# The output projection of a decoder step: from fp32 products to three rounded products, with the residual stream returned later

## The chip, the cores and the metric

The kernel runs on one core of a Trainium2 chip, as one launch. The metric is the device time of the launch in microseconds (us), which is the median of three runs. TensorE multiplies matrices, VectorE, ScalarE and GpSimd do the rest of the arithmetic, and SyncE issues most of the transfers between HBM (the chip's main memory) and SBUF (the memory on the core).

## The reference

A two-layer decoder trunk is computed for 512 prompt tokens and for 8 samples of 4 tokens, 544 rows in all. Every layer projects the normed rows, runs a recurrent memory (mLSTM) and a sparse attention on them, and merges the two by one output projection `w_out` of 1024 by 1024, whose product is added to the residual stream `x`. A gated FFN follows.

```python
for l in range(DEPTH):                       # DEPTH = 2
    mq, mk, mv, mo, mi, mf, aq, ak, av, iq, ik, iw = project(x, g_mix[l], w_in[l])
    m_out, state = mlstm_mixer(mq, mk, mv, mo, mi, mf, ...)      # 512 columns
    a_out = dsa_prompt(...)  # or dsa_sample(...), with paged keys and values; 512 columns
    mix = jnp.concatenate([m_out, a_out], axis=-1)
    x = x + mix @ w_out[l]
    g, u = jnp.split(rmsnorm(x, g_ffn[l]) @ w_gate_up[l], 2, axis=-1)
    x = x + (jax.nn.silu(g) * u) @ w_down[l]
```

## The kernel before

All engines' programs are written out by hand, in order, one function each (`sync_layer`, `pool_layer` for GpSimd, `act_layer` for ScalarE, `tensor_layer`, `vector_layer` for VectorE), and a loop runs them twice, once for each layer. Semaphores are the only thing that holds one engine back for another. `eng.wait_ge(s, n)` waits until semaphore `s` has reached `n`, and `.then_inc(s, 1)` raises it when an instruction is done.

The rows are kept transposed: 8 blocks of 128 features (`KT = 8`) on the partitions, and `T = 544` rows along the free axis, as `x[:, k, t]`. A feature tile of an output is 128 output features by 544 rows. It is summed in two PSUM banks, in two halves of 272 rows.

**Plain fp32 products.** `feature_tile` (line 1064) takes the fp32 weights as they lie in the slab buffer `ring` and the fp32 rows, 8 blocks x 2 halves. In the profile each such product shows as two weight loads and two matmuls, so a tile has 32 matmul records. The 8 tiles of the output projection and the first tile of the down projection are made in this way.

**Three rounded products.** Every other large product splits each operand into a high part, rounded to the type fp32r, and a low part, the whole minus the high part. It sums high x high, high x low and low x high. A tile then has 8 x 3 x 2 = 48 products. `token_chunk` (line 1033) and `conv_tile` (L1049) of the input projection do so, `split_tile` (L1099) of the FFN and `down_tile` (L1080). The weights of the convolution tiles are split by GpSimd: `cast_feature` (L621) writes the high part, `low` (L626) writes the low part over the slab. Those of the FFN are split by VectorE (L1916, L1917).

**Memory.** `ring`, `proj`, `xn`, `cq`, `qk2` and `R4` are fp32 buffers, and `ring_low`, `h_high`, `x_high`, `x_low`, `w_split_even` and `w_split_odd` are the same places in the same order under the type fp32r. `K_PLACE` and `V_PLACE` say where the keys and values of each of the 8 samples are put, 8 pages each.

**Around the output projection.** For each layer the order is:

1. The mixed rows are put into `mixv`, which is `xn`. TensorE turns four heads of the memory (L1437) and four blocks of the attention (`turn_out`, L1426). ScalarE copies the heads out of PSUM (L960) and VectorE the attention (L1888). Both first wait until the results of the layer are stored (`s_stored`).
2. The sample attention runs: `turn_keys` (L1451), `sample_logits` (L1459), `turn_probs`, and `sample_values` (L1489, L1490), which raises `s_s_pv` once for each sample. SyncE loads keys (L552), GpSimd values (L704). After the last keys SyncE issues the return of `x` from its parking place in HBM (L585, 2.2 MB), then the two slabs of `w_out` (L495): slab 8 once all keys are turned, slab 9 once two samples have their values.
3. VectorE scales the last values (L1901), TensorE turns them (L1512), VectorE copies the eight heads of the sample rows into `mixv` (L1905) and raises `s_mix_ready`.
4. TensorE makes the 8 tiles (L1064). After tile m, from m = 2, it adds the sum of squares of tile m-2 (`sum_squares`, L1109). VectorE adds each tile to `x` (L1930) and scales it (L1932), ScalarE squares it (L991). After tile 6 VectorE splits the first FFN weights.

The code that sets the path into step 4 is this:

```python
pe.wait_ge(s_mix_ready, 1)
for m in range(8):
    feature_tile(8 + m // 4, OUT0 + m, P * (m % 4), mixv)
    if m >= 2:
        sum_squares(s_sq2, m - 2)
```

## Time and profile before

| | |
|---|---|
| median of 3 runs | 2156.34 us (2147.86 to 2165.62) |
| the profiled execution, its own time | 2154.16 us |
| its span, first to last instruction | 2152.2 us |
| TensorE busy | 1988.0 us (92%) |
| weight loads of TensorE | 1609.7 us (75%) |
| VectorE busy | 1175.7 us (55%) |
| ScalarE busy | 445.9 us (21%) |
| GpSimd busy | 457.9 us (21%) |
| mean granted clock of TensorE | 0.939 |

The span is 2.0 us shorter than the execution's own time. PE is TensorE's matmuls, PEld its weight loads, DVE is VectorE, ACT is ScalarE, POOL is GpSimd and SPq the queue of SyncE's transfers. The granted clock is a share of the full 2.4 GHz; at 0.5 it is 1.2 GHz. Matmuls are pipelined, so the duration of one record is longer than the distance from one start to the next, and a tile is best read from the start of its first matmul to the start of what comes after it.

### The profile page before, as it was taken

How to read it: one execution, taken by the hardware profiler on the slowest of the kernel's cores; microseconds unless marked ns; L12 is line 12 of the kernel's file. 1: busy time of each engine (PE TensorE's matmuls, PEld its weight loads, DVE VectorE, ACT ScalarE, POOL GpSimd, SP SyncE). 2: the span in 40 equal slices, each digit the busy share in tenths (PEclk: the TensorE clock that was granted, in tenths of full speed). 3: DMA queues.
4: the chain of work that ended last, by engine and by line, in shares of the span. 5: the costliest groups of instructions: out<-in, count | busy, mean ns of one | idle time of the engine just before them, and what ended most of it. 6: DMA issues, size and time to landing. Idle time of an engine off the chain costs nothing. (4 is left out here: it accounts for less than half of the span.)

```text
span 2152.2 us, 31183 instructions
## 1 busy us (share of the span) xinstructions
PE 1988.0 (92%) x11900; PEld 1609.7 (75%) x11900; DVE 1175.7 (55%) x2074; ACT 445.9 (21%) x940; POOL 457.9 (21%) x436
## 2 busy tenths in 40 slices
PE   6999998887999999999969999987889999999997
PEld 5765576744478999989957656766444899999897
DVE  3295975578114454555425779656770155454653
ACT  2123233323202000040022233233331020000400
POOL 2453340034100121200026435201240012121000
PEclk9998988878999999999979999887889999999999
DMA  3320320107511322233232213102172122322332
GB/s 120 120 81 9 93 68 1 55 27 217 183 40 41 116 80 79 79 81 82 55 106 81 81 33 97 40 1 81 53 238 110 40 79 79 108 89 67 81 82 69
DMA packets 183537, 174.32 MB, mean 81 GB/s; under 512 B 30946, under 2 KB 159234, under 8 KB 182866
## 3 DMA queue, kind: packets, MB, share of 16 engines
q1 hardware_dynamic: 178002, 157.55, 23.4%
q0 software_dynamic: 5376, 14.69, 2.2%
q8 instruction: 96, 1.57, 0.3%
q14 instruction: 63, 0.52, 0.1%
HBM read 158.03 MB, written 14.17 MB: 80 GB/s over the span
## 5 line engine op out<-in xcount | busy, mean ns | idle before, releaser
L1099 PE MATMUL psum<-x_high,w_split_even 128*128 128x272 f32 x1408 | 238.5, 289 | 2.3 <-DVE x_low L1938 2.3
L724 POOL TENSOR_TENSOR rawr<-rawr,pen 128x544 f32<-128x544 f32 x44 | 98.4, 2237 | 658.7 <-ACT rawr L1002 658.7
L1099 PE MATMUL psum<-x_high,w_split_odd 128*128 128x272 f32 x1408 | 237.6, 288 | 0.0
L1080 PE MATMUL psum<-h_high,w_split_even 128*128 128x272 f32 x1232 | 204.6, 287 | 1.7 <-issue 1.7
L1099 PEld LDWEIGHTS psum<-x_high,w_split_even 128*128 128x128 f32 x1408 | 199.8, 188 | 3.3 <-issue 3.1
L1099 PEld LDWEIGHTS psum<-x_high,w_split_odd 128*128 128x128 f32 x1408 | 199.6, 188 | 0.0
L1080 PEld LDWEIGHTS psum<-h_high,w_split_even 128*128 128x128 f32 x1232 | 173.4, 188 | 2.5 <-issue 2.5
L1033 PE MATMUL psum<-h_high,x_high 128*128 128x512 f32 (+1 forms) x400 | 168.5, 421 | 0.0
L1033 PE MATMUL psum<-h_high,x_low 128*128 128x512 f32 (+1 forms) x400 | 162.1, 405 | 0.0
L1033 PE MATMUL psum<-ring_low,x_high 128*128 128x512 f32 (+1 forms) x400 | 161.3, 403 | 0.0
L1942 DVE TENSOR_TENSOR rawr<-psum,pen 128x544 f32<-128x544 f32 x44 | 31.9, 725 | 228.1 <-PE psum L1099 215.0
L626 POOL TENSOR_TENSOR ring_low<-ring,h_high 128x512 fp32r<-128x512 f32 (+1 forms) x96 | 153.8, 1603 | 7.7
L1916 DVE CAST w_split_even<-ring 128x256 fp32r<-128x256 f32 (+1 forms) x198 | 98.6, 498 | 99.3 <-PE psum L1080 78.4
L1099 PE MATMUL psum<-x_low,w_split_even 128*128 128x272 f32 x704 | 145.1, 288 | 0.0
L1099 PE MATMUL psum<-x_low,w_split_odd 128*128 128x272 f32 x704 | 145.1, 288 | 0.0
L1002 ACT ACTIVATE rawr<-rawr 128x544 f32<-128x544 f32 x44 | 29.2, 663 | 470.8 <-DVE rawr L1942 470.8
L1064 PE MATMUL psum<-xn,ring 128*128 128x272 f32 x512 | 121.2, 397 | 3.4 <-DVE xn L1905 3.4
L1917 DVE TENSOR_TENSOR w_split_even<-ring,w_split_even 128x256 fp32r<-128x256 f32 (+1 forms) x198 | 119.6, 604 | 6.8
L1064 PEld LDWEIGHTS psum<-xn,ring 128*128 128x128 f32 x512 | 98.2, 192 | 24.4 <-DVE xn L1905 3.9
L1099 PEld LDWEIGHTS psum<-x_low,w_split_odd 128*128 128x128 f32 x704 | 110.6, 189 | 0.0
L1099 PEld LDWEIGHTS psum<-x_low,w_split_even 128*128 128x128 f32 x704 | 110.6, 189 | 0.0
L1033 PEld LDWEIGHTS psum<-h_high,x_high 128*128 128x128 f32 (+1 forms) x400 | 71.6, 179 | 51.7 <-issue 28.9
(375 smaller groups left out, 3575.8 us busy)
## 6 DMA issues: line engine op xcount, KB each, us to landing
ring<-in_w_gate_up_dram SPq DMA_DIRECT2D x44, 1024.0 KB, 7.4
ring<-in_w_in_dram SPq DMA_DIRECT2D x14, 2048.0 KB, 7.9
ring<-in_w_down_dram SPq DMA_DIRECT2D x16, 1408.0 KB, 6.9
ring<-in_w_out_dram SPq DMA_DIRECT2D x4, 2048.0 KB, 8.5
cq<-in_cache_k_dram SPq DMA_DIRECT2D x48, 128.0 KB, 2.0
ring<-in_cache_k_dram SPq DMA_DIRECT2D x48, 128.0 KB, 2.8
x_spill<-x SPq DMA_DIRECT2D x2, 2176.0 KB, 13.3
x<-x_spill SPq DMA_DIRECT2D x2, 2176.0 KB, 11.6
```

The source lines that it names most:

```text
L626: pool.tensor_tensor(out, whole, high.bitcast(F32), ALU.subtract).then_inc(s_w_low, 1)
L724: pool.tensor_tensor(sig(f), sig(f), rstd_ffn.rearrange("p (h t) -> p h t", h=2), ALU.mult).then_inc(s_silu_scaled, 1)
L1002: act.activation(sig(f), sig(f), ACT.Silu).then_inc(s_gate_silu, 1)
L1033: mm = pe.matmul(ps(t)[0:r, :], v[:, k, c:c + r], w, start=(k == 0 and q == 0), stop=(k == KT - 1 and q == 2))
L1064: mm = pe.matmul(out[:, 512 * hf:512 * hf + HALF], w[:, k, c:c + P], src[:, k, HALF * hf:HALF * hf + HALF], start=(k == 0), stop=(k == nk ...
L1080: mm = pe.matmul(out[:, 512 * hf:512 * hf + HALF], down_part(c, w)[:, cols], v[:, HALF * hf:HALF * hf + HALF], start=(k == 0 and q == 0), ...
L1099: mm = pe.matmul(out[:, 512 * hf:512 * hf + HALF], w_part(f, w)[:, k, u, :], v[:, k, HALF * hf:HALF * hf + HALF], start=(k == 0 and q == 0 ...
L1916: step(dve.tensor_copy(high, whole))
L1917: return dve.tensor_tensor(low, whole, high.bitcast(F32), ALU.subtract)
L1942: dve.tensor_tensor(sig(f), halves(FFN0 + 2 * f), rstd2, ALU.mult).then_inc(s_gate_scaled, 1)
```

## The change

- The output projection is made of three rounded products for each block and half (`out_tile`), 384 for a layer in place of 128 fp32 ones.
- Its weights are split by GpSimd (`low_out`), through three buffers in `h_high` (`out_high`). The split of tile m waits for tile m-3.
- The mixed rows lie as a high part (`mix_high`, in `qk2`) and a low part (`mix_low`, in `xn`). ScalarE writes the high parts out of PSUM, for the attention too, and VectorE subtracts them to write the low parts. TensorE's reuse of the PSUM banks now waits for the low parts. For the sample rows VectorE does both, eight small casts and then eight small subtractions.
- `qk2` is thus taken, and so the keys and values that lay there move: the keys of sample 5 to `x`, its values to `R4`, and the values of sample 2 to `x`. The return of `x` from HBM therefore waits for the third sample value and stands behind both slabs of `w_out` in SyncE's queue.
- The FFN's weight buffers change places (`w_part`), and three semaphores become one (`s_prepared`).

```diff
+        mix_high = w_split_even[:, :].rearrange("p (k t) -> p k t", k=KT)
+        mix_low = xh
...
+                sp.wait_ge(s_out_free, OUT0)
                 load_keys(5)
...
-                sp.wait_ge(s_x_parked, 16)
-                sp.dma_start(x[:, :], x_spill).then_inc(s_x_parked, 16)
                 sp.wait_ge(s_kt_turned, 4 * DB)
                 load_slab(8)
                 sp.wait_ge(s_s_pv, 2)
                 load_slab(9)
+                sp.wait_ge(s_x_parked, 16)
+                sp.wait_ge(s_s_pv, 3)
+                sp.dma_start(x[:, :], x_spill).then_inc(s_x_parked, 16)
...
+                def low_out(m):
+                    i = 8 + m // 4
+                    if m % 4 == 0:
+                        slab_arrived(pool, i)
+                    if m == 0:
+                        pool.wait_ge(s_s_log, DB)
+                    elif m == 2:
+                        pool.wait_ge(s_s_pv, 5)
+                    elif m >= 3:
+                        pool.wait_ge(s_out_done, OUT0 + m - 2)
+                    pool.tensor_copy(out_high(m), feature_cols(slab_view(i), m)).then_inc(s_w_high, 1)
+                    low(FEAT0 + 8 + m, feature_cols(slab_view(i), m), out_high(m), feature_cols(slab_low(i), m))
...
-                act.wait_ge(s_c_new, MH)
-                act.wait_ge(s_stored, 16 * STORES)
+                attention_high(0)
+                attention_high(1)
                 for h in range(MH):
                     act.wait_ge(s_mix_turned, h + 1)
-                    act.activation(mixv[:, h, :], ps(2 * (h % 2), 2)[:, 0:T], ACT.Copy).then_inc(s_mix_copied, 1)
+                    act.activation(mix_high[:, h, :], ps(2 * (h % 2), 2)[:, 0:T], ACT.Copy).then_inc(s_mix_copied, 1)
+                attention_high(2)
+                attention_high(3)
...
+                def out_tile(m):
+                    high, low = out_high(m), feature_cols(slab_low(8 + m // 4), m)
+                    pe.wait_ge(s_w_low, FEAT0 + 8 + m + 1)
+                    out = slot(OUT0 + m)
+                    for k in range(KT):
+                        for q, (w, v) in enumerate(((high, mix_high), (high, mix_low), (low, mix_high))):
+                            for hf in range(2):
+                                mm = pe.matmul(out[:, 512 * hf:512 * hf + HALF], w[:, k, :], v[:, k, HALF * hf:HALF * hf + HALF],
+                                               start=(k == 0 and q == 0), stop=(k == KT - 1 and q == 2))
+                    mm.then_inc(s_out_done, 1)
...
                 for h in range(QH):
-                    ins = dve.tensor_copy(mixv[...], ps(1)[...])
+                    whole, high, low = sample_part(h)
+                    ins = dve.tensor_copy(high, whole)
+                step(ins)
+                for h in range(QH):
+                    whole, high, low = sample_part(h)
+                    ins = dve.tensor_tensor(low, whole, high.bitcast(F32), ALU.subtract)
                 ins.then_inc(s_mix_ready, 1)
```

On TensorE the output projection begins behind the last turn of the sample values. Before the change its rows are these (`xn` holds the mixed rows, `ring` the weights):

```order
L1512 MATMUL psum<-con,proj 128x128 [waits s_rows_ready]
L1512 MATMUL psum<-con,proj 128x128
L1064 MATMUL psum<-xn,ring 128x272 [waits out_free,slab_in_even,mix_ready]
L1064 MATMUL psum<-xn,ring 128x272 x15
L1064 MATMUL psum<-xn,ring 128x272 [waits out_free,slab_in_even]
```

After it they are these (`w_split_even` is `mix_high`, `x_high` is `mix_low`, `h_high` and `ring_low` are the two parts of the weights):

```order
L1555 MATMUL psum<-con,proj 128x128 [waits s_rows_ready]
L1555 MATMUL psum<-con,proj 128x128
L1095 MATMUL psum<-w_split_even,h_high 128x272 [waits out_free,w_low,mix_ready]
L1095 MATMUL psum<-w_split_even,h_high 128x272
L1095 MATMUL psum<-x_high,h_high 128x272 x2
L1095 MATMUL psum<-w_split_even,ring_low 128x272 x2
```

The wait for the slab has become one for GpSimd's low part, and 16 instructions of a tile have become 48.

On VectorE the copies of the attention stand between the last scaling of the heads and the picking of the sample keys (L1704), before the change so:

```order
L1880 TENSOR_TENSOR proj<-proj 128x4x128 [waits dve_chain]
L1888 COPY xn<-psum 128x4x128 [waits a_turned,stored,c_copied]
L1888 COPY xn<-psum 128x4x128 [waits a_turned] x3
L1704 MAX small<-pen_s 32x8
L1705 MATCH_REPLACE pen_s<-small,pen_s 32x1056 [waits dve_chain]
```

and after it so:

```order
L1923 TENSOR_TENSOR proj<-proj 128x4x128 [waits dve_chain]
L1933 TENSOR_TENSOR x_high<-psum,w_split_even 128x4x128 [waits a_high,stored,c_copied]
L1933 TENSOR_TENSOR x_high<-psum,w_split_even 128x4x128 [waits a_high]
L1940 TENSOR_TENSOR x_high<-psum,w_split_even 128x544 [waits mix_copied] x4
L1933 TENSOR_TENSOR x_high<-psum,w_split_even 128x4x128 [waits a_high] x2
L1747 MAX small<-pen_s 32x8
```

Four copies have become eight subtractions, each behind a copy of ScalarE's, and the wait for the stores is now VectorE's alone.

On SyncE the return of `x` stood before the slabs of `w_out`:

```order
L552 DMA ring<-in_cache_k_dram 128x256
L585 DMA x<-x_spill 128x4352 [waits x_parked]
L495 ISA [waits out_done,kt_turned]
L495 DMA ring<-in_w_out_dram 128x8x512
L495 ISA [waits out_done,s_pv]
L495 DMA ring<-in_w_out_dram 128x8x512
L492 ISA [waits out_done]
```

and stands behind them now, with a wait of its own:

```order
L558 DMA ring<-in_cache_k_dram 128x256
L501 ISA [waits out_done,kt_turned]
L501 DMA ring<-in_w_out_dram 128x8x512
L501 ISA [waits out_done,s_pv]
L501 DMA ring<-in_w_out_dram 128x8x512
L597 DMA x<-x_spill 128x4352 [waits s_pv,x_parked]
L498 ISA [waits out_done]
```

It moved past two transfers of 2 MB, and the first FFN slab stands behind it as before.

## Rows read from the trace of the kernel before

**Rows 1.** The page: busy time by engine, granted clock in 40 slices.

```profile
PE 1988.0 (92%) x11900; PEld 1609.7 (75%) x11900; DVE 1175.7 (55%) x2074; ACT 445.9 (21%) x940; POOL 457.9 (21%) x436
...
PEclk9998988878999999999979999887889999999999
```

**Rows 2.** Timeline, layer 2, TensorE: start us, us, engine, line, [idle before].

```profile
1664.85 22.27 PE L1064 MATMUL psum<-xn,ring 128*128 128x272 f32 x96 [1.70 <-DVE xn L1905]
...
1687.87 7.50 PE L1064 MATMUL psum<-xn,ring 128*128 128x272 f32 x32
1695.20 1.08 PE L1109 MATMUL psum<-proj,con 128*128 128x272 f32 x4
...
1730.44 0.49 PE L1099 MATMUL psum<-x_high,w_split_even 128*128 128x272 f32 x2 [1.16 <-DVE x_low L1938]
```

**Rows 3.** Windows, layer 1: one convolution tile, one FFN tile, 240 us of FFN.

```profile
core 0: us, PE busy (x) PEld busy (x) DVE busy (x) ACT busy (x) POOL busy (x), PEclk, DMA share, GB/s
263.50:269.60 6.10, 6.10 (x48) 6.04 (x48) 5.83 (x13) 1.64 (x3) 5.94 (x4) 1.00 0.92 304
671.60:677.60 6.00, 5.99 (x48) 6.00 (x49) 4.31 (x7) 4.29 (x7) 0.00 (x0) 1.00 1.01 332
691.00:931.00 240.00, 240.00 (x1918) 240.00 (x1917) 125.34 (x120) 13.26 (x20) 46.15 (x20) 1.00 0.27 86
```

**Rows 4.** Line L1099 of the FFN: one form's weight loads, ns min/median/max.

```profile
L1099 PEld LDWEIGHTS psum<-x_low,w_split_even x704: 187/188/191, 671.8 to 1984.4; 128*128 128x128 f32 x176
```

**Rows 5.** Timeline, VectorE: head copies before the projection, first and last residual adds.

```profile
613.72 0.72 DVE L1930 TENSOR_TENSOR x<-x,psum 128x544 f32<-128x544 f32 x1 [9.45 <-PE psum L1064]
...
1663.19 1.61 DVE L1905 COPY xn<-psum 64x32 f32<-64x32 f32 x8 [0.53 <-PE psum L1512]
1672.56 0.72 DVE L1930 TENSOR_TENSOR x<-x,psum 128x544 f32<-128x544 f32 x1 [7.76 <-PE psum L1064]
...
1728.40 0.72 DVE L1930 TENSOR_TENSOR x<-x,psum 128x544 f32<-128x544 f32 x1 [3.27 <-PE psum L1064]
```

**Rows 6.** Groups by shape, VectorE: a small two-input operation (busy us, mean ns).

```profile
L1718 DVE TENSOR_TENSOR rawr<-psum,x 128x32 f32<-128x32 f32 x16 | 2.9, 182 | 0.0
```

**Rows 7.** Window at the start of layer 1's projection, columns as in rows 3.

```profile
604.30:608.30 4.00, 3.98 (x10) 3.06 (x11) 0.00 (x0) 0.00 (x0) 0.00 (x0) 0.58 0.00 0
```

**Rows 8.** Timeline, layer 2, three engines: rows of heads turned and copied for the projection.

```profile
1563.80 1.29 DVE L1888 COPY xn<-psum 128x512 f32<-128x512 f32 x2
...
1564.56 2.62 PE L1437 MATMUL psum<-con,proj 128*128 128x128 f32 x10 [2.11 <-ACT xn L960]
...
1567.21 0.62 ACT L960 ACTIVATE xn<-psum 128x544 f32<-128x544 f32 x1 [0.66 <-PE psum L1437]
...
1569.11 0.69 DVE L1888 COPY xn<-psum 128x512 f32<-128x512 f32 x1 [0.16 <-PE psum L1426]
...
1570.06 1.73 PE L1451 MATMUL psum<-con,cq 128*128 128x128 f32 x7 [0.99 <-DVE xn L1888]
```

**Rows 9.** Timeline, TensorE: the fifth sample's keys waited for, layers 1 and 2.

```profile
531.53 1.09 PE L1451 MATMUL psum<-con,proj 128*128 128x128 f32 x8 [3.31 <-DMA proj<-in_cache_k_dram]
...
1593.64 1.09 PE L1451 MATMUL psum<-con,proj 128*128 128x128 f32 x8 [1.64 <-DMA proj<-in_cache_k_dram]
```

**Rows 10.** Groups by shape, GpSimd: the split of one convolution tile's weights.

```profile
L626 POOL TENSOR_TENSOR ring_low<-ring,h_high 128x1024 fp32r<-128x1024 f32 x16 | 39.0, 2435 | 1.3
L621 POOL CAST h_high<-ring 128x1024 fp32r<-128x1024 f32 x16 | 18.1, 1129 | 104.8 <-PE psum L1049 62.3 <-PE psum L1033 42.4
```

**Rows 11.** Page and timeline of layer 2: transfers and the third sample's value.

```profile
ring<-in_w_out_dram SPq DMA_DIRECT2D x4, 2048.0 KB, 8.5
...
x<-x_spill SPq DMA_DIRECT2D x2, 2176.0 KB, 11.6
...
1616.44 19.04 SPq L495 DMA_DIRECT2D ring<-in_w_out_dram  x2
...
1638.40 0.61 PE L1490 MATMUL psum<-proj 32*32 32x256 f32 x2
```

More of the change, by code:

```diff
@@ L392, in halves_of @@
             return [buf[:, c:c + 2048] for c in (0, 2048)]
-        (first0, first1), (cq0, cq1), (qk0, qk1) = (halves_of(buf) for buf in (ring[:, 0:4096], cq, qk2))
+        (first0, first1), (cq0, cq1), (x0, x1) = (halves_of(buf) for buf in (ring[:, 0:4096], cq, x))
         spare0, spare1 = proj[:, 5392:7440], proj[:, 3344:5392]
-        K_PLACE = (cq0, cq1, first0, first1, spare0, qk0, cq0, first0)
-        V_PLACE = halves_of(ring[:, 4096:8192]) + halves_of(R4) + [spare1, qk1, cq1, spare0]
+        K_PLACE = (cq0, cq1, first0, first1, spare0, x0, cq0, first0)
+        (odd0, odd1), (r0, r1) = halves_of(ring[:, 4096:8192]), halves_of(R4)
+        V_PLACE = (odd0, odd1, x1, r1, spare1, r0, cq1, spare0)
         def k_pages(b):
@@ L412, in w_part @@
         def w_part(f, part):
-            w = (w_split_even if f % 2 == 0 else w_split_odd)[:, 2048 * part:2048 * part + 2048]
+            w = (w_split_odd if f % 2 == 0 else w_split_even)[:, 2048 * part:2048 * part + 2048]
             return w.rearrange("p (k u c) -> p k u c", k=KT, u=2)
@@ L457, in feature_high, with out_high @@
             at = 400 + 1024 * (m % 3)
+            return h_high[:, at:at + 1024].rearrange("p (k n) -> p k n", k=KT)
+        def out_high(m):
+            at = (400, 1424, 3344)[m % 3]
             return h_high[:, at:at + 1024].rearrange("p (k n) -> p k n", k=KT)
@@ L719, in _ @@
                 load_values(7)
+                for m in range(8):
+                    low_out(m)
                 pool.wait_ge(s_rstd2, 1)
@@ L1440, in _ @@
                 turn_out(3)
[L1441 removed]
+                pe.wait_ge(s_mix_low, MH)
                 pe.wait_ge(s_s_q_ready, 1)
@@ L1885, in _, with attention_low @@
                 dve.wait_ge(s_stored, 16 * STORES)
-                for j in range(4):
-                    dve.wait_ge(s_a_turned, j + 1)
-                    dve.tensor_copy(mixv[:, 4:8, P * j:P * j + P], ps(4 + j % 2).rearrange("p (f t) -> p f t", f=4)).then_inc(s_a_copied, 1)
+                def attention_low(j):
+                    dve.wait_ge(s_a_high, j + 1)
+                    cols = slice(P * j, P * j + P)
+                    dve.tensor_tensor(mix_low[:, 4:8, cols], ps(4 + j % 2).rearrange("p (f t) -> p f t", f=4),
+                                      mix_high[:, 4:8, cols].bitcast(F32), ALU.subtract).then_inc(s_a_copied, 1)
+                attention_low(0)
+                attention_low(1)
+                for h in range(MH):
+                    dve.wait_ge(s_mix_copied, h + 1)
+                    dve.tensor_tensor(mix_low[:, h, :], ps(2 * (h % 2), 2)[:, 0:T], mix_high[:, h, :].bitcast(F32), ALU.subtract).then_inc(s_mix_low, 1)
+                attention_low(2)
+                attention_low(3)
                 for _ in range(TOPK_S // 8 - PICKS_CONV - PICKS_TURN - len(PICKS_MEM)):
@@ L1902, in _, with sample_part @@
                 dve.wait_ge(s_s_rows_turned, 1)
-                for h in range(QH):
-                    p, src, dst = h // 4, HD * (h // 2 % 2), HD * (h % 2)
-                    ins = dve.tensor_copy(mixv[dst:dst + HD, 4 + h // 2, SEQ:T].rearrange("p (g b t) -> p g b t", g=2, b=4),
-                                          ps(1)[src:src + HD, :].rearrange("p (g q b c) -> p g q b c", g=2, q=2, b=4)[:, :, p, :, DT * h:DT * h + DT])
+                def sample_part(h):
+                    p, src, dst = h // 4, HD * (h // 2 % 2), HD * (h % 2)
+                    whole = ps(1)[src:src + HD, :].rearrange("p (g q b c) -> p g q b c", g=2, q=2, b=4)[:, :, p, :, DT * h:DT * h + DT]
+                    high, low = (buf[dst:dst + HD, 4 + h // 2, SEQ:T].rearrange("p (g b t) -> p g b t", g=2, b=4) for buf in (mix_high, mix_low))
+                    return whole, high, low
+                for h in range(QH):
+                    whole, high, low = sample_part(h)
[4 more added lines that the diff above has]
+                    ins = dve.tensor_tensor(low, whole, high.bitcast(F32), ALU.subtract)
                 ins.then_inc(s_mix_ready, 1)
```

27 lines of the change are left out of this document (14 added, 13 removed).

## The prediction

> **What bounds the kernel now.** I read the page first. TensorE is busy for 92% of the span and no other engine for more than 55% [rows 1], so a saving counts if it shortens TensorE's own work or its waits, and added work elsewhere counts where TensorE waits for it. Then I read the timeline of TensorE through the output projection [rows 2]. From 1664.85 us on, tile follows tile with no idle time named between them. A tile lasts from 1687.87 to 1695.20, 7.33 us, and from the third tile on a sum of squares follows it, whose record is 1.08 us long. Only two waits frame the stage: 1.70 us at its start for VectorE's last copy, and 1.16 us at its end for the first low part of the FFN's rows. The stage is bound by TensorE's matmuls, and its length is 8 tiles plus those sums. So the question is what a tile costs in the other form, and what the new splitting puts on the path ahead of the first tile.
>
> **The tile in three products.** The form is in the trace twice. Convolution tile 0 has the same 48 products of 128x272, its weights split by GpSimd into the same two buffers, and takes 6.1 us for 48 records while all four other engines work and the transfers stand at 0.92. The first FFN tile has 48 in 6.00 us, and the FFN runs 1918 of them in 240.0 us, 0.125 us each [rows 3]. So 48 x 0.125 = 6.0 us against 7.33 us: 1.33 us for a tile, 10.6 us for a layer, **21.3 us** for both. It all lies on the path, since the stage has no other bound. The bounds of a tile are 6.00 and 6.1 us, so the gain is 19.7 to 21.3 us.
>
> The weight loads speak against this at first sight. One takes 188 ns [rows 4], longer than the 125 ns from product to product, so the loads must overlap the matmuls before them, and in the FFN they do. The Trainium skill (TensorE: Matmul & The Clock Gate, Part 3, The mechanism) says that a weight load overlaps matmuls in flight only when its group of array rows differs, which is not so here, as each product uses the whole array. By that rule the tiles would get slower; by the rows they get faster, and the rows are of this very form. I keep the row and give the rule a small chance below.
>
> **Is everything there when TensorE asks?** GpSimd's split of one tile is 1.13 + 2.44 = 3.6 us [rows 10]. The first tiles are split during the sample values: slab 8 is issued at 1616.44 and lands some 8.5 us later [rows 11], 40 us ahead of the first tile. From tile 3 on, the split may start when tile m-3 ends and is needed two tiles later, 12.0 us; 3.6 us fit with 8.4 us to spare. The split would have to take more than three times as long to be felt. VectorE's work for a tile and GpSimd's now start on the same event, but the add must only be done one tile, 6.0 us, later. Cost: nothing.
>
> The return of x waits for the third sample value, which ends at 1638.40 + 0.61 = 1639.0. The second slab leaves at about 1635, is 8.5 us under way, and if x follows strictly behind it, 11.6 us more, it lands at 1655 [rows 11]. VectorE asks for it at its first residual add, now 1672.56 [rows 5]. That leaves 17 us. The next slab stands behind it in the queue, but waits for tile 3 anyway. Cost: nothing; it costs microsecond for microsecond if x came more than 17 us later. The wait that is set before the keys of sample 5 is for the last convolution tile, which is read long before those loads are reached behind 24 other pages, so it costs nothing either.
>
> **Ahead of the first tile.** The eight head copies take 1.61 us [rows 5], and TensorE waits for the last. Eight casts take their place, and then eight subtractions with an input from PSUM. No row shows them at 64x32. The nearest is 0.18 us for a subtract-like operation of 128x32 from PSUM [rows 6], the copies are spaced by 0.20. So 8 x 0.15 to 8 x 0.25 = 1.2 to 2.0 us for a layer; with the wait between the two groups I take 1.7 us. It is all on the path, 3.4 us for both layers.
>
> **The clock.** In layer 1 the granted clock was 0.58 over the first 4.0 us of the projection [rows 7], that is mostly the level of 1.2 GHz, after the idle 1.7 us. The first add came after a wait of 9.45 us there and of 7.76 us in layer 2 [rows 5], where the same idle time did no harm. So a start at the lower level costs 1.7 us. The idle stretch before the first tile now doubles from 1.7 to 3.4 us, and I take it that both layers start low: **+1.7 us**, with -1.7 (neither) and +5.1 (both, for twice as long) as bounds. The Trainium skill (TensorE: Matmul & The Clock Gate, Why this matters for your kernels) warns of just such idle gaps between bursts of matmuls; by it too both layers would start low.
>
> **The mixed rows.** In layer 2 the stores let go at 1563.80. ScalarE and VectorE copied at the same time, and TensorE turned the third head at 1564.56 [rows 8]. Now VectorE must first do two attention parts and one head part, 0.65 + 0.65 + 0.7 = 2.0 us, before the third head may be turned: 1.3 us later than before. At the end a copy of 0.62 by ScalarE comes before VectorE's last part, some 0.7 us more. So the turning of the keys begins 2.0 us later than 1570.06. What hides it is the next wait: TensorE stands idle for the fifth sample's keys for 3.31 us in layer 1 and 1.64 us in layer 2 [rows 9], and these keys come at SyncE's own pace, which nothing here delays. So nothing is lost in layer 1 and 2.0 - 1.64 = 0.4 us in layer 2. Without that cover it would be 2.0 us for each layer, 4.0 us in all; and if the shorter wait in layer 1 spares a clock fall, 1.6 us come back. **+0.4 us**, bounds -1.6 and +4.0.
>
> **At the end of the projection** VectorE splits the first FFN weights during tile 7. Tile 7 is now shorter by 1.33 us; the last add waited 3.27 us for TensorE behind that split [rows 5], and would wait 1.9 us now. The FFN changes only the names of its buffers.
>
> **Sum**, against the profiled execution's own 2154.16 us: -21.3 + 3.4 + 1.7 + 0.4 = -15.8, so **2138.4 us**. That execution lies 2.2 us below the median of the runs, 2156.34.
>
> **Rivals.**
>
> *The covers fail.* The rows' chain costs its full 4.0 us, the small subtractions 4.0 and the clock 5.1: -21.3 + 13.1 = -8.2, 2146 us. For it: the cover in layer 2 is short, and the order of three engines there is new. Against it: three things must go wrong together. Chance 0.12.
>
> *The clock is kind.* Neither layer starts low, the wait for the keys loses its fall, the subtractions take 1.2 us: -21.3 + 2.4 - 1.7 - 1.6 = -22.2, 2132 us. For it: in layer 2 an idle 1.7 us did no harm. Against it: the idle stretch doubles. Chance 0.14.
>
> *Weight loads in line, slower than before.* If a product lasted as long as its load, a tile would be 48 x 0.188 = 9.0 us, 1.7 more than now: 16 x 1.7 + 5.5 = +32.7, 2187 us. The mechanism sits in TensorE's queue at every product. It decides from the spacing at which 16 tiles lose what they gain: 7.33 less 5.5/16 us, over 48, is 0.146 us; above that the kernel is slower. Against it stand 0.125 in the FFN and in the convolution tile [rows 3]. Chance 0.03.
>
> *x comes late.* The first residual add, and two tiles later TensorE, stand for it. It takes a landing 17 + 15.8 us later than worked out to make the kernel slower than before. The window in which it travels has no other load than one slab. Chance 0.03.
>
> That the products are not the rounded ones is excluded by the order of instructions, which shows 48 short ones for a tile on the fp32r buffers.
>
> **How the numbers follow.** The forecast case has 0.68, with 2135 to 2143 as its own range. The bounds of the unknown costs reach from 2132 to 2146. The runs of before spread by 8.5 below and 9.3 above their median, so a median moves by some 3 us: 2130 to 2149. About 1% is what a measurement of this kernel can tell from no change, that is 21.5 us. The forecast lies at 0.7%. The kind clock and a lucky median of the forecast case give faster 0.19; slower takes the loads, a late x and the far end of the measurement, 0.06; 0.75 remains for the same.
>
> **What the profile after would show.** Tile starts 6.0 us apart, plus 1 with a sum, and a projection of some 53 us from its first product to the last; the idle time before it near 3.4 us; a clock near 0.6 in its first 4 us in both layers; idle for the fifth sample's keys of 1.3 us in layer 1 and none in layer 2; the first add not waiting for x; no wait of TensorE for GpSimd. The prediction is wrong if a tile takes over 6.3 us, if TensorE waits for a low part of the weights, or if the key stage starts over 3 us later.

## The result, and the profile after

The changed kernel took 2153.82 us as a median of 20 runs (2133.29 to 2176.4), the kernel before, on the same chips, 2167.73 us as a median of 20 (2147.86 to 2192.91). The ratio is 0.9921, with a 95% interval of 0.9892 to 0.995; it compares the fast executions alone, and between the two medians of all 20 it is 0.9936. The change is worth 0.6% to 0.8%, as forecast (2138.4 over 2154.16 is 0.9927), but the time itself lies 15.4 us above the forecast and 4.8 us above its range. The kernel before had been met too low: its three runs had a median of 2156.34 us, its 20 runs have one of 2167.73.

The profiled execution of after has an own time of 2145.2 us, 9.0 less than that of before, and a mean granted clock of 0.931 against 0.939. Its page:

```profile
span 2143.6 us, 31763 instructions
...
PE 1977.1 (92%) x12156; PEld 1614.7 (75%) x12156; DVE 1189.7 (56%) x2098; ACT 450.7 (21%) x948; POOL 512.5 (24%) x468
...
PEclk9998998867999999999979999887889999999999
...
ring<-in_w_out_dram SPq DMA_DIRECT2D x4, 2048.0 KB, 8.5
...
x<-x_spill SPq DMA_DIRECT2D x2, 2176.0 KB, 9.9
```

Beside [rows 1], TensorE has 256 more matmuls and is busy 10.9 us less, GpSimd is busy 54.6 us more. In the row of the clock the slices nine and ten, 429 to 536 us, read 6 and 7 where they read 7 and 8, and slice six reads 9 where it read 8. The change touches only the end of the two, from 490 us on, and nothing of slice six.

TensorE ahead of the projection and in its first tile, layer 2 and then layer 1 (start us, us, engine, line, tile, count, idle before):

```profile
1665.77 0.82 PE L1095 MATMUL psum<-w_split_even,h_high 128*128 128x272 f32 x2 [3.33 <-DVE x_high L1970]
1666.39 0.66 PE L1095 MATMUL psum<-x_high,h_high 128*128 128x272 f32 x2
...
1668.66 0.42 PE L1095 MATMUL psum<-w_split_even,h_high 128*128 128x272 f32 x2
1668.92 0.42 PE L1095 MATMUL psum<-x_high,h_high 128*128 128x272 f32 x2
...
608.96 0.82 PE L1095 MATMUL psum<-w_split_even,h_high 128*128 128x272 f32 x2 [3.33 <-DVE x_high L1970]
...
664.04 1.08 PE L1152 MATMUL psum<-proj,con 128*128 128x272 f32 x4
...
666.28 0.49 PE L1142 MATMUL psum<-x_high,w_split_odd 128*128 128x272 f32 x2 [1.16 <-DVE x_low L2002]
```

A record of two products is followed by the next after 0.25 us at full clock, 0.125 us a product, and after 0.45 us in the first 3 to 5 us, where the clock is at or near the level of 1.2 GHz: over the first 4 us it was 0.50 in layer 1 and 0.64 in layer 2. The wait ahead of the stage is 3.33 us in both layers, 1.70 before [rows 2]. The projection lasts 57.3 us in layer 1, from its first product to the first of the FFN.

VectorE ahead of the first tile and at the residual adds of layer 1:

```profile
605.66 1.61 DVE L1966 CAST w_split_even<-psum 64x32 fp32r<-64x32 f32 x8 [0.53 <-PE psum L1555]
607.30 1.60 DVE L1970 TENSOR_TENSOR x_high<-psum,w_split_even 64x32 fp32r<-64x32 f32 x8
617.57 0.72 DVE L1994 TENSOR_TENSOR x<-x,psum 128x544 f32<-128x544 f32 x1 [8.66 <-PE psum L1095]
...
623.50 0.72 DVE L1994 TENSOR_TENSOR x<-x,psum 128x544 f32<-128x544 f32 x1 [4.63 <-PE psum L1095]
...
629.50 0.72 DVE L1994 TENSOR_TENSOR x<-x,psum 128x544 f32<-128x544 f32 x1 [4.57 <-PE psum L1095]
...
664.24 0.72 DVE L1994 TENSOR_TENSOR x<-x,psum 128x544 f32<-128x544 f32 x1 [1.98 <-PE psum L1095]
```

The adds are 5.9 and 6.0 us apart, the last one waits 1.98 us (forecast 1.9, [rows 5]), and all of them wait for TensorE, none for `x`.

The clearest view of where the time went is a table of stages, from the start of a stage's first matmul to the start of the next one's (us, layer 1 | layer 2, read from TensorE's timeline). "Mix and turn" runs from the turning of the memory's keys to the first products of the memory's new state, "rows" up to the turning of the first sample's keys. "FFN" holds the first, plain tile of the down projection too, and "down" of layer 2 ends with TensorE's last matmul.

| kernel | input projection | convolution, attention | mix and turn | rows | keys | values | output projection | FFN | down |
|---|---|---|---|---|---|---|---|---|---|
| before | 231.1 229.0 | 150.4 150.4 | 72.4 72.4 | 21.2 22.2 | 58.6 56.5 | 38.2 38.2 | 67.3 65.6 | 288.8 288.8 | 135.5 127.8 |
| after | 229.4 232.6 | 143.9 150.4 | 83.9 72.4 | 24.6 24.0 | 54.8 55.3 | 39.9 39.9 | 57.3 56.3 | 288.8 288.8 | 136.2 127.9 |

The four stages that the change touches (rows, keys, values, output projection) sum to 367.8 us before and 352.2 us after, before rounding: **-15.7 us**, forecast -15.8. The first three stages, which it does not touch, sum to 905.8 and 912.5 us: **+6.6 us**. The remainder to the -9.0 of the own times, +0.1, lies in the down projection and at the edges of the span. The forecast plus these 6.6 us is 2145.0 us, beside the 2145.2 us of the profiled execution.

These 6.6 us come from single stages that take another length for the same work. Windows over mix and turn of layer 1, before and then after (the columns are those of rows 3, and the sum's are PE, PEld, DVE, ACT, POOL):

```profile
413.90:438.00 24.10, 21.44 (x158) 19.36 (x156) 13.73 (x24) 6.38 (x10) 6.50 (x4) 0.71 0.42 120
438.00:458.00 20.00, 18.67 (x50) 8.09 (x50) 14.20 (x28) 4.43 (x14) 7.19 (x10) 0.75 0.09 26
458.00:478.00 20.00, 16.00 (x65) 9.59 (x64) 16.68 (x35) 5.67 (x23) 5.90 (x10) 0.91 0.00 1
...
sum 72.40, PE 63.46 PEld 41.88 DVE 48.08 ACT 17.34 POOL 19.92; mean PE 15.87 PEld 10.47 DVE 12.02 ACT 4.34 POOL 4.98
```

```profile
405.70:430.00 24.30, 21.41 (x158) 19.33 (x156) 13.93 (x25) 6.38 (x10) 6.73 (x4) 0.71 0.41 120
430.00:450.00 20.00, 19.38 (x30) 7.41 (x31) 11.27 (x19) 3.35 (x7) 5.92 (x7) 0.50 0.09 25
450.00:470.00 20.00, 18.69 (x56) 11.56 (x55) 11.38 (x25) 4.22 (x20) 4.01 (x9) 0.66 0.00 1
...
sum 83.90, PE 75.47 PEld 49.42 DVE 48.08 ACT 17.34 POOL 19.92; mean PE 18.87 PEld 12.36 DVE 12.02 ACT 4.34 POOL 4.98
```

VectorE, ScalarE and GpSimd are busy for the same 48.08, 17.34 and 19.92 us. TensorE needs 12.0 us more for the same matmuls, since its granted clock is 0.50 and 0.66 where it was 0.75 and 0.91.

### The profile page after: what moved, and what is told of

Its sections match the earlier page's. It is cut to its first block and busy times, and to the rows that moved or that the text cites. A ratio compares the mean times of both kernels' runs of the same rounds, so it can differ in the third digit from the quotient of the medians.

```text
span 2143.6 us, 31763 instructions
## 1 busy us (share of the span) xinstructions
PE 1977.1 (92%) x12156; PEld 1614.7 (75%) x12156; DVE 1189.7 (56%) x2098; ACT 450.7 (21%) x948; POOL 512.5 (24%) x468
## 3 DMA queue, kind: packets, MB, share of 16 engines
q8 instruction: 98, 1.61, 0.3%
## 5 line engine op out<-in xcount | busy, mean ns | idle before, releaser
L634 POOL TENSOR_TENSOR ring_low<-ring,h_high 128x512 fp32r<-128x512 f32 (+1 forms) x112 | 192.8, 1722 | 9.0
L617 POOL CAST h_high<-ring 128x512 fp32r<-128x512 f32 x80 | 62.6, 783 | 162.5 <-PE psum L1064 155.5
L1064 PEld LDWEIGHTS psum<-ring_low,x_high 128*128 128x128 f32 (+1 forms) x400 | 72.0, 180 | 25.2
```

What stands on the lines that cost most here:

```text
L617: pool.tensor_copy(chunk_high(s, k), slab_view(1 + s)[:, k, :]).then_inc(s_w_high, 1)
L634: pool.tensor_tensor(out, whole, high.bitcast(F32), ALU.subtract).then_inc(s_w_low, 1)
L1064: mm = pe.matmul(ps(t)[0:r, :], v[:, k, c:c + r], w, start=(k == 0 and q == 0), stop=(k == KT - 1 and q == 2))
```

## The experiments

Two theories stand against each other on the level. **Theory:** the change does what was worked out, and the absolute time was missed because the executions first seen were ones with a high clock in stages that the change leaves alone. **Rival:** the change costs something there, through the new places of keys and values, or through what GpSimd and the clock do later. For most terms of the sum there is a run as well. Runs of one chip share their runs of before; 58 of these were made on four chips beside the experiments. Experiments 3 to 6 have one execution for each kernel (2122.36, 2194.3, 2155.35, 2160.81 and 2149.02 us, in the order below), so they are read by their stages.

**1. Both kernels again, unchanged.**

> The kernel before, unchanged. Theory A (the absolute level moves with the granted clock in stages that the change does not touch): its median lies nearer to 2167 us than to 2156, its ratio to the kernel before is 1.00 within 0.5%, its runs spread by 20 us or more, and within one kernel a run with a lower mean granted clock is a longer run. In its profile the projection takes 65 to 67 us from its first product to the first FFN product in both layers, as before. Theory B (the profiled run of 2154 us was typical, and the 11.5 us that the memory stage of layer 1 took longer in the changed kernel's profile are a cost of the change): the median is near 2155 and the memory stage of layer 1, from the turning of the keys to the last memory products, takes 72 us again.

> The changed kernel, unchanged. Theory A: ratio 0.990 to 0.995; the projection again takes 56 to 58 us for a layer up to the first FFN product and 39.9 us from the first sample value to the first product, while the memory stage of layer 1 comes out at another length than the 83.9 us of the first profile, anywhere from 72 to 85 us. Theory B: the memory stage of layer 1 takes 84 us again.

Before took 2176.3 us (median of 12, 2163.04 to 2191.94), beside 2173.27 of 29 runs of the same kernel: ratio 1.0047, 1.0006 to 1.0089. So the measured ratio of a kernel to itself can be off by 0.5%, and here even the interval leaves out 1. After took 2153.71 us (12 runs), ratio 0.9931, 0.989 to 0.9973. In the stages:

| kernel | input projection | convolution, attention | mix and turn | rows | keys | values | output projection |
|---|---|---|---|---|---|---|---|
| before again | 226.3 232.4 | 157.3 156.9 | 77.5 83.9 | 22.0 21.9 | 59.0 56.4 | 38.2 38.2 | 67.3 67.3 |
| after again | 234.9 229.5 | 143.8 150.4 | 83.9 83.9 | 24.6 24.6 | 54.8 54.8 | 39.9 39.9 | 57.3 57.3 |
| places only | 232.8 232.3 | 143.9 143.8 | 83.9 83.9 | 21.7 21.6 | 56.7 56.8 | 38.2 38.2 | 67.3 67.3 |
| early start | 227.4 231.2 | 157.3 150.4 | 77.5 72.4 | 24.4 25.0 | 55.9 56.4 | 38.2 38.2 | 55.3 55.3 |

The first three stages of before sum to 905.8 us in the first profile and to 934.4 in this one, 28.5 us more for the same program. In these profiles they come in steps: about 144, 150.4 or 157 for the convolution and attention, 72.4, 77.5 or 83.9 for mix and turn, in either kernel. The touched stages hardly move: 370.4 us against 367.8 for before, 353.2 against 352.2 for after. Between the two new profiles the change is worth -17.2 us.

One expectation was missed. Mix and turn of layer 1 was to come at another length in the changed kernel, and it came at 83.9 us again, as the rival had it. What speaks against the rival is the kernel before: it took 77.5 and 83.9 us there in its second profile, and 83.9 us in layer 1 with the places of experiment 2, where the products are the old ones. Two profiles of before are too few to say that the changed kernel takes the long length no more often.

**2. Only the places of keys and values, and the late return of `x`.** The rest is the kernel before.

```diff
-        K_PLACE = (cq0, cq1, first0, first1, spare0, qk0, cq0, first0)
+        K_PLACE = (cq0, cq1, first0, first1, spare0, x0, cq0, first0)
...
+                sp.wait_ge(s_x_parked, 16)
+                sp.wait_ge(s_s_pv, 3)
+                sp.dma_start(x[:, :], x_spill).then_inc(s_x_parked, 16)
```

> The kernel before with only the moved places of keys and values, the wait ahead of the keys of sample 5, and the return of x behind both slabs of w_out and the third sample value; the products stay fp32. Theory A: no difference, ratio 0.997 to 1.003, the projection stage at 65 to 67 us, the first residual add does not wait for x. Rival (the moves cost something that the products' gain hides): ratio above 1.003, by a wait for keys or for x.

2174.33 us, ratio 1.0026, 0.997 to 1.0081: no difference. Rows and keys together take 78.4 us in each layer, where before had 79.8 and 81.0 in layer 1 and 78.7 and 78.3 in layer 2, so the places save 1.3 to 2.6 us in layer 1 and cost nothing. The projection has no trace of the later `x` (67.3 us). The rival falls for this part of the change.

**3. The product as the price of a tile.** The product of high weights and low rows is left out.

```diff
-for q, (w, v) in enumerate(((high, mix_high), (high, mix_low), (low, mix_high))):
+for q, (w, v) in enumerate(((high, mix_high), (low, mix_high))):
```

> The changed kernel without the product of the weights' high part and the rows' low part: 32 products for a tile, so part of the result is left out. Theory A (0.125 us for a product, and nothing but TensorE bounds the stage): a tile takes 4.0 us and the projection up to the first FFN product falls from about 57 to about 41 us, if GpSimd's split of 3.6 us still fits into two tiles of 4.0. Rival (weight loads or GpSimd's splits set the pace): the stage falls by less than 12 us, with a wait of TensorE for GpSimd.

The projection took 41.4 us in both layers, 15.9 less than 57.3. That is 128 products fewer, 0.124 us each.

**4. The cover of GpSimd's split.** In the first kernel the split of tile m waits for tile m-1, in the second for tile m-2, in place of m-3.

```diff
                     elif m >= 3:
-                        pool.wait_ge(s_out_done, OUT0 + m - 2)
+                        pool.wait_ge(s_out_done, OUT0 + m)
```

> The changed kernel, but from tile 3 on GpSimd starts a tile's split only when the tile before it is done, two tiles later than it could. Theory A: TensorE now waits for each of tiles 3 to 7 for the whole split, 3.5 to 3.8 us each, 18 us for a layer, and the stage goes from 57 to about 75 us; that prices the cover of the split. Rival (the split is faster or slower beside TensorE alone than in the convolution tiles): another number.

> GpSimd's split of tile m waits for tile m-2 in place of m-3, so that one tile of 6 us (7 with a sum) remains for a split of 3.6 us. My theory: 2.4 us of slack remain, the projection stays at 56 to 58 us. Rival (events and queues take over 2.4 us on each hand-over): 5 tiles each lose what is over, and the projection is 2 us or more longer.

The first: a projection of 77.7 us, 20.4 more, and the timeline of TensorE names the cause, a wait for GpSimd at the start of each tile from tile 3 on (here tiles 3 and 4):

```profile
631.96 0.52 PE L1095 MATMUL psum<-w_split_even,h_high 128*128 128x272 f32 x2 [2.73 <-POOL ring_low L634]
...
643.50 0.82 PE L1095 MATMUL psum<-w_split_even,h_high 128*128 128x272 f32 x2 [2.80 <-POOL ring_low L634]
```

The five waits sum to 13.7 us, 2.7 to 2.8 each, where 3.5 to 3.8 each were expected. The tile at 643.50 also starts with the long records (0.82) of the low clock, so the waits cost more than their length. The second: 57.3 us in both layers. With one tile less of cover nothing is lost, so at least 6 of the 8.4 us of slack were there.

**5. The small subtractions, twice.**

```diff
                     ins = dve.tensor_tensor(low, whole, high.bitcast(F32), ALU.subtract)
+                step(ins)
+                for h in range(QH):
+                    whole, high, low = sample_part(h)
+                    ins = dve.tensor_tensor(low, whole, high.bitcast(F32), ALU.subtract)
```

> Every one of the eight small head subtractions ahead of the first tile is made twice (the second time after a wait for the first eight, same values). My theory: they lie whole on the path, 1.6 us for eight plus about 0.1 for the wait, so the stretch from the first sample value to the first product of the output projection goes from 39.9 to 41.6 us in each layer, and the projection itself stays at 56.3 to 57.3 us. Rival (the wait for the group of casts and not the subtractions makes the second 1.6 us): the stretch stays within 0.3 us of 39.9. The whole time is not expected to tell 3.4 us.

The values stage took 41.5 us in both layers, 1.6 more than 39.9, and the rival is out. VectorE's timeline has the three groups in a row:

```profile
608.13 1.60 DVE L1966 CAST w_split_even<-psum 64x32 fp32r<-64x32 f32 x8 [0.53 <-PE psum L1555]
609.76 1.60 DVE L1970 TENSOR_TENSOR x_high<-psum,w_split_even 64x32 fp32r<-64x32 f32 x8
611.40 1.60 DVE L1974 TENSOR_TENSOR x_high<-psum,w_split_even 64x32 fp32r<-64x32 f32 x8
```

**6. The return of `x` later still**, behind the eighth sample value.

```diff
-                sp.wait_ge(s_s_pv, 3)
+                sp.wait_ge(s_s_pv, 8)
```

> The return of x waits for the eighth sample value in place of the third, some 20 us later. My theory: x's transfer of 9.9 us then starts about 5 us ahead of the first tile and lands about as VectorE asks for it at its first residual add, 12 us after: the first add is at most 2 us later, TensorE does not notice since it needs the banks only two tiles later, and the projection stays at 56 to 58 us. Rival (x is close to the edge already, and the slabs in the queue hold it up): the projection lasts over 60 us, with VectorE's first add waiting for a transfer.

57.3 and 57.1 us, and the first add still waits for TensorE. SyncE issues the transfer at 602.40, it takes 8.7 us, and the add comes 13 us after the issue, so 4 us of margin are left:

```profile
602.40 0.34 SPq L597 DMA_DIRECT2D x<-x_spill  x1
...
615.37 0.72 DVE L1994 TENSOR_TENSOR x<-x,psum 128x544 f32<-128x544 f32 x1 [8.70 <-PE psum L1095]
```

**7. The clock at the start.** Seven products with `ones`, which are no part of the computation, fill the wait ahead of the first tile.

```diff
+                for _ in range(7):
+                    pe.matmul(ps(6)[:, 0:HALF], ones, con[:, 0:HALF], start=True, stop=True)
                 pe.wait_ge(s_mix_ready, 1)
```

> The changed kernel with seven fp32 products of 128x272 into a free bank while TensorE waits for the head casts and subtractions, about 3.2 us of work at 2.4 GHz. Theory A (the idle gap takes the clock down at the start of the projection): the clock stays at 1.00 over the first tile in both layers, and the first residual add comes 1.5 to 1.8 us earlier relative to the last turn of the sample values, 3 us in all. Rival (the clock falls for another reason, or the fillers run at the lower level and delay the first product): no gain or a loss of up to 3 us.

The projection took 55.1 us in both layers, 2.2 and 1.2 less than in the two layers of after, which start low. The first tile runs at full clock from its first product:

```profile
616.64 3.37 PE L1560 MATMUL psum<-con 128*128 128x272 f32 x14
620.14 0.52 PE L1095 MATMUL psum<-w_split_even,h_high 128*128 128x272 f32 x2
620.50 0.42 PE L1095 MATMUL psum<-x_high,h_high 128*128 128x272 f32 x2
620.75 0.42 PE L1095 MATMUL psum<-w_split_even,ring_low 128*128 128x272 f32 x2
```

The whole, 2159.22 us with a ratio of 0.9895 (0.9846 to 0.9944), cannot show 4 us.

**8. An early start.** The first tile takes all its products with the high part of the rows first, and waits for the small subtractions only before the last third. To get there the turned rows go to another PSUM bank.

```diff
+parts = ((high, mix_high), (low, mix_high), (high, mix_low))
+steps = [(k, q) for q in range(3) for k in range(KT)] if m == 0 else [(k, q) for k in range(KT) for q in range(3)]
+for n, (k, q) in enumerate(steps):
+    if m == 0 and n == 2 * KT:
+        pe.wait_ge(s_mix_ready, 2)
```

> The changed kernel, but the first tile does its 32 products with the high part of the rows first, so that it starts after the eight casts and the eight subtractions run beside it (the turned sample values lie in another bank). Theory A: the idle time before the first product falls from 3.33 to about 1.7 us, which gives 1.6 us for a layer, and where the clock no longer falls another 1.7: 3 to 7 us less than the changed kernel in its own stage, ratio to the kernel before about 0.990. Rival (the subtractions were hidden, or the clock falls anyway and costs more because the first tile is then at the lower level): no gain against the changed kernel.

> The early start once more, beside the two kernels below. My theory (what the kernel does at TensorE's waits moves its mean granted clock, and the time follows that clock at 15 to 20 us for each 0.01): time 2145 us at a clock of 0.930, and the two below lie lower on the same line at a higher clock. Rival (the clock is the chip's and the execution's own affair; the high clock of 0.936 in the run before was chance): all three kernels have the same mean clock within 0.002.

The values stage is back at 38.2 us, and the projection came at 55.3 us twice in the first profile, at 56.7 and 58.0 in the second. Times: 2146.57 us, ratio 0.9889 (0.9805 to 0.9973), and 2144.61 us, ratio 0.986 (0.9801 to 0.9918). Values and projection together take 93.5 us a layer in the first profile, against 96.9 on the average of the four layers of after: 3.4 less. In the second profile it is 1.3 less, since both projections start low.

**9. Can a kernel set the level?** Seven fillers at the waits of mix and turn; then with the early start; then with three more of 128x256 ahead of the first tile.

```diff
+                for _ in range(3):
+                    pe.matmul(ps(0)[:, 0:HALF], ones, con[:, 0:HALF], start=True, stop=True)
                 pe.wait_ge(s_c_copied, 1)
```

> The changed kernel with seven fp32 products of 128x272 at three places in front of the memory stage and before the heads are turned, where TensorE waits 3 to 4 us each. Theory A (the run's level is set by how long the clock stays at 1.2 GHz in the convolution and memory stages, whose lengths come out at 72.4, 77.5 or 83.9 us for the same instructions): fillers change how often the clock falls there, the stage more often takes 72 us, and the median falls by some us. Rival (the clock falls there whatever the waits are, as the small products of that stage do not hold it): the stage still takes 77 to 84 us and the fillers cost 0 to 5 us for a layer.

> Two earlier edits together: the first tile starts on the high parts alone, and seven filler products keep TensorE busy over the waits of the memory stage. They are not part of the computation. My theory: sample values 38.2 and projection 55.3 us as with the early start alone, and the memory stage at its short lengths, 70 to 78 us, where the kernel after has 72.4 or 83.9; the time is 2140 us (ratio 0.987, 3 to 10 us below the early start alone). Rival (the memory stage's length is drawn from execution to execution whatever is done at its waits): the stage comes at 77.5 or 83.9 as often as without the filler, and the ratio equals that of the early start alone, 0.989.

> The seven fillers at the waits of the memory stage together with the early start, again. My theory: mean clock 0.003 to 0.006 above that of the early start alone in this same set, time 5 to 10 us below it. Rival: same clock within 0.002, and a time within 3 us of it, since the fillers do nothing for the result and only take what was idle.

> As above, with three more filler products (128x256) in the 1.7 us that TensorE waits for the head casts ahead of the first tile; none of the fillers is part of the computation. My theory: the projection keeps full clock from its first product in both layers, 55.1 to 55.3 us, where it came at 58.0 and 56.7 without this filler; mean clock equal to or above that of the fillers in the memory stage alone, time 0 to 4 us lower. Rival (the clock at the projection's start depends on what came long before): the projection still comes at 56 to 58 us in one of the layers.

| kernel | time us | ratio to before | mean clock, before's beside it | mix and turn | output projection |
|---|---|---|---|---|---|
| fillers in mix and turn | 2156.34 | 0.9897 (0.9846 to 0.9948) | 0.927, 0.923 | 69.6 77.5 | 57.8 57.2 |
| early start and these | 2137.02 | 0.9833 (0.9775 to 0.9891) | 0.936, 0.930 | 77.5 83.8 | 58.0 56.7 |
| the same again | 2155.56 | 0.9891 (0.9835 to 0.9947) | 0.927, 0.929 | 83.8 77.4 | 56.7 56.6 |
| and the gap filled | 2148.41 | 0.9886 (0.9831 to 0.9941) | 0.931, 0.929 | 72.4 77.4 | 55.3 55.3 |

After one set I took the fillers for a real gain through the clock. The second set, made to decide it, went against that: on the same chip the early start alone had 0.930 and 2144.61 us, with the fillers 0.927 and 2155.56 us. My theory fell. The rival's numbers (the same clock within 0.002, a time within 3 us) were not met either, as the kernel with the fillers came out 0.003 lower and 11 us longer. What stands, as far as six runs of each can tell, is that the fillers give no reliable gain, and that the high clock of the first set was most likely chance. One thing holds: the three fillers in the short wait ahead of the projection. Of the eight starts with an idle 1.7 us there (early start, with or without fillers elsewhere), six ran low and two did not. With the wait filled, here and in experiment 7, none of four did:

```profile
600.91 1.46 PE L1568 MATMUL psum<-con 128*128 128x256 f32 x6
602.77 2.27 PE L1099 MATMUL psum<-w_split_even,h_high 128*128 128x272 f32 x16 [0.40 <-DVE w_split_even L1978]
604.88 2.17 PE L1099 MATMUL psum<-w_split_even,ring_low 128*128 128x272 f32 x16
```

Sixteen products take 2.0 to 2.1 us from the very first on. By its stages the early start is the best version, with or without this filling. Its five ratios overlap, 0.9833 to 0.9891, and their intervals overlap with those of after.

**What the level is made of.** Over the 58 runs of before the time follows the mean granted clock of the execution, with a correlation of -0.97: 19 us for each 0.01 of clock, and 2169.0 us at 0.930. For the 20 runs of after it is 17.7 us for 0.01 and 2146.8 us at 0.930. At the same mean clock the two kernels thus lie 22 us apart, while the stages give 15.7 and 17.2. Part of this must be so: the change takes away 19.2 us of products, nearly all at full clock, which by itself lowers the mean clock by 0.0006, or 1 us on this line (my estimate). The rest is open. A single run of before has a standard deviation of 10.5 us, and medians of three drawn from these runs have one of 7.1 us. Only 3 of the 58 runs are as low as 2156.34 us, and only 0.5% of all triples drawn from them have a median that low.

## Why the prediction was right, and where it was wrong

**The step that failed** is the one from three runs to a level: "The runs of before spread by 8.5 below and 9.3 above their median, so a median moves by some 3 us". A median of three moves by 7 us here, and the one at hand lay 11.4 us below that of 20 runs. The forecast added its sum to a profiled execution that lay lower still, with the short length of 72.4 us for mix and turn in both layers and a clock of 0.939. That base of 2154.16 us is 13.6 us below the 2167.73 of the 20 runs, and makes 13.6 of the 15.4 us that the forecast is off. Three runs 17.8 us apart say little about their middle. Their own standard deviation is 8.9 us, which makes some 6 us for a median of three (my estimate, for a bell curve), twice what was put in. With the 7.1 us found since, 1.28 x 7.1 = 9 us (four fifths of a bell curve lie within 1.28 standard deviations) belong on either side of the 2132 to 2146 that the costs reached to: 2123 to 2155, which just holds the time. That the level was low could not be read from one profile; it took the same program again. A median of three as low as the first is rare among the 58 later runs, so the first three may have had more in common than chance, and no run here shows what.

That the sum over the touched stages meets the forecast to 0.1 us is luck in the last digit. Tile and clock gave -19.2 for -19.6, the small subtractions 3.3 for 3.4, the mixed rows +0.3 for +0.4; and the second pair of profiles gives -17.2.

**The tile** was right. Products lie 0.125 us apart with weight loads of 188 ns, and leaving one out of three saves 0.124 us each. The projection shrank from 67.3 and 65.6 us to 57.3 and 56.3, 19.2 us in all. Where both kernels start at full clock, it is 65.6 against 55.1 to 55.3, 10.3 to 10.5 us a layer for a forecast of 10.6. For the profiles at hand the terms said 21.3 less 1.7 for the clock, 19.6. The rule of the Trainium skill (TensorE: Matmul & The Clock Gate, Part 3, The mechanism), that a load overlaps only when its row group differs, does not hold for this form: with 128x128 loads of 188 ns at every product of the projection the spacing stayed at 125 ns. The prediction took this sentence alone; a few lines above it the same section also lets a load run ahead when it goes to the background weight buffer. That would fit these rows, but no run here shows where a load goes. The rival is out.

**The small subtractions** cost 1.60 us plus 0.03 for the wait between, and the values stage grew by 1.6 us, where 1.7 were put in. Doubling them cost 1.6 us again.

**The clock at the start** was low in both layers of after, as expected: 57.3 and 56.3 us against 55.1 with the wait filled, 1.2 to 2.2 us a layer. The term of +1.7 holds against the profile that it was made for. In general before starts low as well, in five of the six projections seen (67.3 against 65.6), so against a usual execution this term is near zero. It did not show in the ratio.

**The mixed rows.** The turning of the keys waits 1.61 us for the low part, and rows grew by 3.4 and 1.8 us where 2.0 were forecast. Keys shrank by 3.8 and 1.2 us, since the waits for the fifth sample's keys [rows 9] went: in layer 1 there is none left at all, where I expected 1.3 us:

```profile
536.12 1.09 PE L1494 MATMUL psum<-con,proj 128*128 128x128 f32 x8
537.46 1.15 PE L1494 MATMUL psum<-con,proj 128*128 128x128 f32 x8 [0.25 <-ACT proj L998]
```

The sum is -0.3 and +0.6, +0.3 in all for a forecast of +0.4. That the cover would hold was the main doubt of the rival "the covers fail", and it held. One sign of being wrong did come, though: the prediction was to be wrong if the key stage started over 3 us later, and in layer 1 it started 3.5 us later. It cost next to nothing, since the wait behind it was 3.31 us. Half of the miss lies in the first profile of before, where rows took 21.2 us. Between the second profiles, with 22.0 and 21.9 us before and 24.6 after, the delay is 2.6 and 2.8.

The traces also show why the wait went. SyncE issues the first of these keys 33.6 us after the start of rows in layer 1 of before and 33.8 us in after, so they keep their own pace and TensorE comes later to them. And behind the wait before lay a fall of the clock that after does not have. These are the 5 us from the fifth sample's first product, layer 1, before and then after (columns as in rows 3):

```profile
531.53:536.53 5.00, 4.75 (x19) 2.54 (x20) 4.86 (x7) 2.29 (x4) 2.56 (x5) 0.68 0.83 230
```

```profile
536.12:541.12 5.00, 4.75 (x23) 2.37 (x23) 4.86 (x7) 2.18 (x4) 2.15 (x4) 1.00 0.79 234
```

The clock was 0.68 there (0.50 in before again) and 1.00 in after, which is the clock fall that the prediction had as a bound and not in its sum. With the places alone the wait in layer 1 was 1.85 us, against 3.31 and 2.89 in two executions of before. There TensorE had a clock of 0.76 in the first 8 us of the key stage where before had 1.00 both times, and reached these keys 1.2 us later.

**GpSimd and x** cost nothing, as put in. `x` left at 1638.40 in layer 2, was 9.9 us under way and was asked for at 1673.45. The margin is 25 us and not 17, although the second slab, issued at 1634.40 and some 8.5 us under way, still travelled when `x` left: the transfer of `x` did not begin only when the slab had landed.

**"The clock is kind"** was the rival with 0.14. The lowest of the 20 runs of after, 2133.29 us, comes near its 2132 us, but by the level and not by the change.

## What to carry to other kernels

A forecast of a change and a forecast of a time are two things: sum the change over the stages that it touches, and give the base a spread of its own from what a few runs and their mean granted clocks allow. When a stage is compared between two profiles, look first at stages that the change leaves alone; if these differ, with equal busy time on the other engines, the clock is at work. A chain that gets longer on the way to a wait for something else is free as long as it is shorter than that wait, and a short wait of TensorE ahead of a dense stage is worth filling: 1.2 to 2.2 us for each start here.

## What was not expected of the hardware

- The same instructions of one stage take 72.4, 77.5 or 83.9 us, from one execution to the next and from layer to layer. The differences are close to steps, and the granted clock in 20 us windows goes with them (0.50 to 0.91). Another stage took about 144, 150.4 or 157 us in most profiles; over all kernels here it lies between 139.9 and 161.2.
- On one chip, one program's time moved by 47 us (2142.39 to 2189.55) over 29 runs. Over 58 runs on four chips it lay along a line of 19 us for each 0.01 of mean granted clock. Fillers at the waits did not move that level reliably.
- An idle 3.3 us ahead of dense products was followed by the level of 1.2 GHz in all 14 layers that have this wait (after, after again, and experiments 3, 4, 6 and the fillers in mix and turn alone), with a clock of 0.50 to 0.52 over the first 3 us. An idle 1.7 us was followed by a low start in 11 of 14 (0.50 to 0.68), and in 3 the clock stayed at 1.00.
